# Three-product matmuls: a chunk's twelve matmuls issued product by product instead of tile by tile

## The reference, cut to what matters

```
proj = h @ w_in                       # block 1: 2048 x 10,688
u = (y_rwkv * silu(z_rwkv)) @ w_br_rwkv
out = merged @ w_out
mix_out = einsum("bsm,md->bsd", mixed, w_out[i]) + b_out[i]
hid = silu(einsum("bsd,df->bsf", x, w_gate[i])) * einsum("bsd,df->bsf", x, w_up[i])
ffn = einsum("bsf,fd->bsd", hid, w_down[i])
u = h @ w_up                          # block 3: 2048 x 11,008
return (silu(gate) * val) @ w_down    # block 3: 5504 x 2048
```

## Time and profile before

| what | value |
|---|---|
| time, median of 3 runs | 3628.6 us |
| the profiled execution's own time | 3629.15 us |
| its span in the profile | 3627.8 us |
| TensorE matmul busy | 3493.5 us (96%) |
| TensorE weight load busy | 3318.2 us (91%) |
| VectorE, ScalarE, GpSimd busy | 2297.4, 1451.5, 76.8 us |
| DMA | 655.24 MB, mean 181 GB/s |
| mean granted TensorE clock | 0.987 |

### The profile page before, as it was taken

The page is one execution under the profiler, slowest core; times in us unless marked ns, Lnnn a source line. Parts: engine busy times, 40 slices in busy tenths (PEclk is TensorE's granted clock), DMA queues, the critical chain, the costliest instruction groups (busy, mean ns, idle before and its releaser), DMA issues.

```text
span 3627.8 us, 64316 instructions
## 1 busy us (share of the span) xinstructions
PE 3493.5 (96%) x26426; PEld 3318.2 (91%) x26426; DVE 2297.4 (63%) x3100; ACT 1451.5 (40%) x1733; POOL 76.8 (2%) x156
## 2 busy tenths in 40 slices
PE   8999999999999999989999999989998899999998
PEld 8997888988889884989999999979988899999998
DVE  7775755545558768767755554555566677777545
ACT  5441233223224301554444434444445544444443
POOL 0000100000000000000000000000000000000000
PEclk9999999999999999999999999999999999999999
DMA  8657611111137773657755555535443455555554
GB/s 325 251 193 306 238 61 49 52 65 69 61 127 270 291 270 131 218 191 285 285 199 187 194 199 198 198 107 182 151 156 106 153 187 186 186 187 185 189 187 151
DMA packets 91876, 655.24 MB, mean 181 GB/s; under 512 B 10193, under 2 KB 10833, under 8 KB 13138
## 3 DMA queue, kind: packets, MB, share of 16 engines
q1 hardware_dynamic: 74736, 540.05, 41.0%
q0 software_dynamic: 14400, 104.86, 7.5%
q10 hardware_dynamic: 2594, 8.15, 0.6%
HBM read 650.93 MB, written 2.10 MB: 180 GB/s over the span
## 4 chain that ended last, share of the span: by engine, by line
PE 83%; DVE 9%; ACT 3%; DMA 3%; issue 2%; DVEq 1%; ACTq 0%; SPq 0%
PE ps L465 20%; PE ps L466 19%; PE ps L467 19%; PE ps L631 6%; DMA work<-in_ada 2%; PE ps L426 2%; PE ps L706 2%; PE ps L694 2%; PE ps L436 1%; DVE ring_parts L1627 1%; DVE work L1642 1%; DVE work L2007 1%; PE ps L511 1%; PE ps L750 1%; PE ps L741 1%
## 5 line engine op out<-in xcount | busy, mean ns | idle before, releaser
L1627 DVE TENSOR_TENSOR ring_parts<-ring,ring_hi 128x1024 fp32r<-128x1024 f32 x858 | 1032.3, 1223 | 723.9 <-ACT ring_hi L1083 710.5
L1083 ACT ACTIVATE ring_hi<-ring 128x1024 fp32r<-128x1024 f32 x858 | 901.6, 1059 | 1159.6 <-PE ps L467 1107.8
L466 PE MATMUL ps<-h_lo,ring_hi 128*128 128x256 f32 x2624 | 732.5, 279 | 0.0
L465 PE MATMUL ps<-h_hi,ring_hi 128*128 128x256 f32 x2112 | 595.0, 282 | 14.5 <-DVE h_lo L1649 8.5
L467 PE MATMUL ps<-h_hi,ring_parts 128*128 128x256 f32 x2112 | 589.9, 279 | 0.0
L466 PEld LDWEIGHTS ps<-h_lo,ring_hi 128*128 128x128 f32 x2624 | 494.7, 189 | 1.4 <-issue 1.2
L465 PE MATMUL ps<-x_hi,ring_hi 128*128 128x256 f32 x1664 | 465.5, 280 | 6.1 <-DVE x_lo L1649 4.5
L466 PE MATMUL ps<-x_lo,ring_hi 128*128 128x256 f32 x1664 | 461.9, 278 | 0.0
L467 PE MATMUL ps<-x_hi,ring_parts 128*128 128x256 f32 x1664 | 460.2, 277 | 0.0
L465 PEld LDWEIGHTS ps<-h_hi,ring_hi 128*128 128x128 f32 x2112 | 398.3, 189 | 17.3 <-issue 10.1
L467 PEld LDWEIGHTS ps<-h_hi,ring_parts 128*128 128x128 f32 x2112 | 398.7, 189 | 0.0
(11 more groups left out here) (450 smaller groups left out, 5724.3 us busy)
## 6 DMA issues: line engine op xcount, KB each, us to landing
ring<-in_weights SPq DMA_DIRECT2D x511, 1024.0 KB, 4.8
work<-in_ada POOLq DMA_DIRECT2D x96, 1024.0 KB, 7.2
work<-in_c_row POOLq DMA_DIRECT2D x4, 1024.0 KB, 6.0
resid<-in_lora ACTq DMA_DIRECT2D x9, 256.0 KB, 3.6
resid<-in_x SPq DMA_DIRECT2D x4, 512.0 KB, 6.6
resid<-in_x ACTq DMA_DIRECT2D x1, 2048.0 KB, 14.2
out<-work SPq DMA_DIRECT2D x4, 512.0 KB, 2.8
con<-in_const ACTq DMA_DIRECT2D x1, 1536.0 KB
```

The source lines that it names most:

```text
L465: mm(o, w_hi[:, k, cols], hi(kc), start=(kc == 0 and m % 2 == 0), stop=False, skip_group_check=True)
L466: mm(o, w_hi[:, k, cols], lo(kc), start=False, stop=False, skip_group_check=True)
L1083: A(high_ring(n)[:, 2 * (e % 2) + half, :], ring[:, n % RING, half * (SLOT // 2):(half + 1) * (SLOT // 2)], ACT.Copy)\
L1627: tt(lo, x, high_ring(n)[:, e % 4, :].bitcast(F32), ALU.subtract).then_inc(S("lo_ready"), 1)
```

## The change

Within a chunk the loop over the four tiles is run three times: first all four rounded products, then all four with the remainder weights, then all four with the remainder features. Before, each tile's three products stood together, with the remainder feature ahead of the remainder weight. The waits ahead of the chunk and the semaphore given by the half's last matmul stay where they are.

```diff
-                        for m in range(4):
-                            o = PS[:, b + m // 2, (m % 2) * T:(m % 2 + 1) * T]
-                            cols = slice(m * P, (m + 1) * P)
-                            mm(o, w_hi[:, k, cols], hi(kc), start=(kc == 0 and m % 2 == 0), stop=False, skip_group_check=True)
-                            mm(o, w_hi[:, k, cols], lo(kc), start=False, stop=False, skip_group_check=True)
-                            ins = mm(o, w_lo[:, 2 * half + k, cols], hi(kc), start=False, stop=(kc == last - 1),
+                        out = [PS[:, b + m // 2, (m % 2) * T:(m % 2 + 1) * T] for m in range(4)]
+                        cols = [slice(m * P, (m + 1) * P) for m in range(4)]
+                        for m in range(4):
+                            mm(out[m], w_hi[:, k, cols[m]], hi(kc), start=(kc == 0 and m % 2 == 0), stop=False,
+                               skip_group_check=True)
+                        for m in range(4):
+                            mm(out[m], w_lo[:, 2 * half + k, cols[m]], hi(kc), start=False, stop=False, skip_group_check=True)
+                        for m in range(4):
+                            ins = mm(out[m], w_hi[:, k, cols[m]], lo(kc), start=False, stop=(kc == last - 1),
                                      skip_group_check=True)
                     ins.then_inc(S("half_used") if half == 0 else w_used, 1)
```

## The result

| | before | after |
|---|---|---|
| median, us | 3623.79 (3613.96 to 3633.73, 4 runs) | 3654.11 (3650.01 to 3655.87, 4 runs) |
| profiled execution's span, us | 3627.8 | 3654.6 |
| ratio | | 1.0082, 95% interval 1.005 to 1.0114 |

The change made the kernel slower by 0.8%. The forecast of 3628 us and no change was wrong. The time is that of the prediction's rival C, priced there at 3657 us.

A forecast was written before the change was run, and what follows sets the result against it. TensorE was taken as the bound: number of matmuls times spacing of starts. Terms 0 + 0 + 0 on the profiled 3629.15 us, 0.55 us above the median, rounded to 3628 us; eight-in-ten range 3585 to 3660 us.

The forecast's parts named there:

- rival C: TensorE's matmuls all run at 0.1178 us under the new order: 12,700 x 0.0022 = 28 us slower, 3657 us; chance 0.18.
- Instructions and waits: Per chunk, same matmuls, weight loads and semaphores, and no engine queued differently behind the waits: 0 each.
- PSUM and the moving operand: In the chunk loop, switching output tile at each matmul and keeping the features longer were each worth 0.
- The stationary operand: In the chunk loop, no longer using a stationary tile twice in a row loses nothing: 0.
- the step into L466: Start spacing onto the matmul reusing L465's stationary tile: 0.12 us, never ffn2's short one, so repeating gains 0.
- tight: The faster of two levels for 256-column float32r matmuls, seen in ffn2 and down2: 0.1156 us each.
- What sets the pace: TensorE's 0.1156 us per matmul is the columns' streaming pace, 0.00045 us per column, which an order cannot change.
- The 0.109 us: Skill's spacing for 256 columns at full clock; reaching it would save an estimated 139 us, but the traced spacing decides.
- The wide level as a matter of history: Stages fall into 0.1156 or 0.1178 us with the same code; ffn3 and down3 were at 0.1178; range 3613 to 3645.
- the eight-in-ten range: Whole kernel time, 3585 to 3660 us: the forecast's range, all of rival C and the small end of a faster rival.

The follow-up runs named there:

- e5: Changed kernel's stationary and moving operand order, but output tiles as in the kernel before (three in a row to one tile): 3651.15 us, ratio 1.0094.
- e6: Kernel before, stationary and moving operands unchanged, but each matmul writes another output tile than its predecessor: 3615.73 us, ratio 1.0004.
- e7: Changed kernel's stationary tiles and outputs, but the moving operand as before (every third matmul takes remainder features): 3653.04 us, ratio 1.009.
- e8: Kernel before, but the moving operand as in the change (eight matmuls with rounded features, then four with remainders): 3625.38 us, ratio 1.0012.
- e1: Kernel before, tile by tile, but remainder weight ahead of remainder feature, so no stationary tile repeats: 3616.72 us, ratio 0.9981; timed again, ratio 0.9986.
- e9: Kernel before, column blocks unchanged, but stationary buffers as in the change (four ring_hi, four ring_parts, four ring_hi): 3654.56 us, ratio 1.01.
- e10: Kernel before, buffers unchanged (ring_hi, ring_hi, ring_parts), but the column block steps with every matmul: 3615.61 us, ratio 1.0002.
- e12: Kernel before, but all stationary tiles from ring_hi and the column block stepping with every matmul: 3647.72 us, ratio 1.0069.
- e15: Kernel before, but all stationary tiles from ring_parts and the column block stepping with every matmul: 3673.08 us, ratio 1.0135.
- e17: The kernel before, unchanged, profiled a second time: 3615.04 us.
- e2: Kernel before, but per tile the rounded product then remainder feature, and afterwards remainder weight for all four tiles: 3654.69 us, ratio 1.0084.
- e3: Changed kernel's product-by-product order, but remainder features second and remainder weights last: 3654.16 us, ratio 1.0087.
- e11: Kernel before, but the third product also takes the rounded weight, so one ring_hi tile is loaded three times running: 3653.61 us, ratio 1.0104.

## Why the prediction was wrong

*Instructions and waits: right.* Counts are equal, the wait for the remainder weights stayed small (14.0 to 10.4 us), no other engine became the bound.

*PSUM and the moving operand: right for the level, and now shown in ffn2.* Both were taken at 0. e5 and e6 give the outputs no effect on the level, e7 and e8 the moving operand none. (w_out3 differed by 1 ns over 768 matmuls, under 1 us.)

*The stationary operand: wrong. This is the step that failed.* It asked only whether a repeated tile is cheaper, and answered with 0. e1 confirms that repetition is worth nothing. But the change also turns the buffers' sequence from a regular three (H H L) into a twelve (8 H, 4 L, taken round the chunk), and that was never asked. With e9 and e10 it is this sequence that carries the whole 0.8%. The term put at 0 is 2.2 ns for each of the some 12,700 matmuls that were tight, 28 us. The reason given for the 0, that the step into L466 is never the short one, misread the pattern: in ffn2 the short step of 112.5 ns is the second one after the buffer turns to `ring_parts`, before the change (onto L465) as in e1 (onto the remainder feature's product, on the same output tile).

*"What sets the pace": wrong.* The tight 0.1156 us was read as the pace of the columns, since 512 columns took twice as long. e12, in its profiled execution, ran nearly 800 us of matmuls of the same shapes at 0.1134, below that "pace", and e15 at 0.1187. A pace that an order or an address can change is not that of the columns. The two column counts agreed, but both came with a pattern of three, so they were no two independent witnesses. The 0.109 us that the prediction takes from the Trainium skill was reached nowhere (the lowest is 0.1133). In "TensorE: Matmul & The Clock Gate", section "Back-to-back issue gap", it is given for a matmul by itself and not for a stream of weight loads and matmuls.

*The wide level as a matter of history: half right.* For the kernel before it is (e17): the level varied between executions. For the change it is not: in its profile no stage is tight (w_out3 is lowest, 117.3), its four runs lie within 6 us, and e2, e3, e5, e7 and e9 with the same sequence of buffers are at 117.8 in ffn2 and ffn3 in every profile.

*Rival C: right in size, thin in mechanism.* It put 12,700 x 0.0022 = 28 us on the wide level throughout and 3657 us; the form's steps grew by 27.4 us and the time is 3654.11. The 28 us hold against an execution with ffn3 wide, as the profiled one was. Against the kernel before in the later comparisons, with medians near 3617, the same sequence of buffers costs 33 to 38 us (e2, e3, e5, e7, e9). That the eight-in-ten range, 3585 to 3660, holds 3654 is owed to C's place in it and not to the forecast. One of its two guesses, that a group of twelve keeps the pattern from settling, is what the runs support; the other, the second load of w_hi apart from the first, is refuted by e1. It deserved more than 0.18: the wide level was seen holding for 700 us, while nothing showed that a pattern other than three could be tight.

What stays open is the mechanism below the pattern. That steps stray around the loads from `ring_parts` (115.8, 112.5, 116.7, 123.3, 120.0 ns) and come back to near 118 is seen; that this straying throws the sequence out of the tight level in each chunk is my reading, not shown. What the unit of 6.67 ns is was not tried either, nor why a constant sequence of buffers (e11, e12) was never at 115.6. The Trainium skill says, in "TensorE: Matmul & The Clock Gate", section "Step-by-step: what each phase is for", that loading the next tile's weights does not take read bandwidth from the running matmul. The runs can't say whether bandwidth is what is lost, but they disagree with the reading that the source of a hidden load is free: e12 and e15 differ in nothing but the buffer of the stationary tiles, and a matmul takes 113.4 and 118.7 ns in ffn2 of their profiles and 117.8 and 118.7 in ffn3.

## What to carry to other kernels

Where TensorE streams float32r matmuls back to back, measure the spacing of starts stage by stage from windows with counts, and do it in more than one profile: the same code may run at two levels 2% apart, and here only patterns of three over the two buffers were ever at 0.1156 us. Judge such a kernel by many executions, since one profile shows one of its states. Reordering for fewer changes of operand or output bought nothing. The order rounded, remainder weight, remainder feature tile by tile (e1) was never above 3623.14 us in 22 runs, against 24 of 86 above 3625 for the kernel before. It is the version to keep, for some 0.15% in the median, which the intervals only just tell from none.

## What was not expected of the hardware

The spacing of float32r matmuls changed with the buffers that their stationary tiles come from and the order of these, though each matmul has its weight load in every version (26426 of each). At a full granted clock and with no wait, 256 columns took 0.1133, 0.1156, 0.1167, 0.1178, 0.1187, 0.1189 or 0.1200 us, steady over whole stages, and each repeating group of steps took a whole number of units of 6.67 ns. And one program held either of two such levels in the same stage in two executions, 0.1156 or 0.1178 us in ffn3, which makes 14 us of 3614.
